# A two-layer decoder block: the last MLP slice as a plain product, the shared key and query gains folded into the weights, and the first attention's maxima as spare contraction rows

## The reference

```python
def _fox_attention(h, w_in, b_f, g_q, g_k, w_out):        # layer 0, 16 heads of 64
    proj = h @ w_in                                       # q, k, v and a gate per head
    q, k = _rmsnorm(q, g_q), _rmsnorm(k, g_k)
    c = cumsum(log_sigmoid(gate + b_f))
    s = q @ k.T * 64 ** -0.5 + c[t] - c[s]                # causal
    return softmax(s) @ v @ w_out

def _shared_kv(h, g_kv, w_kv, g_k):                       # after layer 0
    kv = _rmsnorm(h, g_kv) @ w_kv                         # 128 key and 128 value columns

def _swa_sink_attention(h, w_q, g_q, k_band, v_band, ...) # layer 1, 16 heads, window 128
    q = _rmsnorm((h @ w_q).reshape(...), g_q)
    ...                                                   # scores with bias and sink, softmax, @ v

def _sq_relu_mlp(h, w_up, w_down):
    return square(relu(h @ w_up)) @ w_down                # 1024 -> 4096 -> 1024

for layer in range(2):
    h = h + attention(_rmsnorm(h, g_attn[layer]), ...)    # fox in layer 0, sliding window in layer 1
    h = h + _sq_relu_mlp(_rmsnorm(h, g_mlp[layer]), w_up[layer], w_down[layer])
```

## Time and profile before

| | |
|---|---|
| executions timed | 1196.8, 1198.57 and 1202.5 us, median 1198.57 us |
| the profiled execution | 1199.23 us, of which the span of the trace is 1197.4 us |
| PE busy | 1147.1 us, 96% of the span |
| DVE, POOL, ACT busy | 908.0, 736.2 and 619.5 us |
| mean granted TensorE clock | 0.989 |

### The profile page before, as it was taken

One profiled execution on the slowest core, in us unless ns is written; L12 is line 12 of the kernel. 1 busy time (PEld: TensorE's weight loads), 2 busy tenths in 40 slices (PEclk: granted clock), 3 DMA queues, 4 the chain that ended last, 5 costly groups with the idle time before them and its releaser, 6 DMA issues.

```text
span 1197.4 us, 14655 instructions
## 1 busy us (share of the span) xinstructions
PE 1147.1 (96%) x5282; PEld 942.9 (79%) x5282; DVE 908.0 (76%) x991; ACT 619.5 (52%) x880; POOL 736.2 (61%) x489
## 2 busy tenths in 40 slices
PE   7999999998999999999987799998999999999996
PEld 6778788877888888888865588887888888888884
DVE  6678788866587876877699778876577768776878
ACT  3458788854444444444433588874354344444432
POOL 5515434415588788878856333324487888788856
PEclk9999999998999999999999899999999999999999
DMA  7221211112432423242133201111424233323121
GB/s 242 72 71 36 71 35 35 65 41 71 166 98 88 141 75 118 89 139 73 36 105 106 71 18 54 36 36 47 137 99 141 71 109 102 123 89 100 41 71 71
DMA packets 88498, 101.46 MB, mean 85 GB/s; under 512 B 3640, under 2 KB 68336, under 8 KB 88432
## 3 DMA queue, kind: packets, MB, share of 16 engines
q1 hardware_dynamic: 88224, 100.37, 25.7%
q10 hardware_dynamic: 208, 0.23, 0.1%
HBM read 98.47 MB, written 2.12 MB: 84 GB/s over the span
## 4 chain that ended last, share of the span: by engine, by line
PE 74%; issue 9%; POOL 8%; DVE 7%; ACT 2%; DMA 0%; POOLq 0%; DVEq 0%; ACTq 0%
PE ps L1640 22%; PE ps L1642 22%; PE ps L1641 22%; POOL w_lo L569 4%; PE ps L2110 2%; POOL fox_sq_lo L576 2%; DVE m_nat L1385 1%; DVE xn_lo L1133 1%; POOL ring_lo L613 1%; PE ps L1817 1%; POOL w_lo L613 1%; ACT w_hi L669 1%; PE ps L2073 1%; PE ps L2092 0%; PE ps L2095 0%
## 5 line engine op out<-in xcount | busy, mean ns | idle before, releaser
L613 POOL TENSOR_TENSOR w_lo<-d_raw,w_hi 128x512 fp32r<-128x512 f32 x160 | 253.8, 1613 | 70.3 <-ACT w_hi L862 70.3
L1640 PE MATMUL ps<-xn_hi,w_hi 128*128 128x512 f32 x480 | 192.0, 400 | 2.9 <-DVE xn_lo L1133 2.9
L569 POOL TENSOR_TENSOR w_lo<-stage,w_hi 128x512 fp32r<-128x512 f32 x80 | 119.1, 1520 | 116.6 <-ACT w_hi L669 116.6
L1642 PE MATMUL ps<-xn_hi,w_lo 128*128 128x512 f32 x480 | 187.6, 391 | 0.0
L1641 PE MATMUL ps<-xn_lo,w_hi 128*128 128x512 f32 x480 | 187.3, 390 | 0.0
L862 ACT ACTIVATE w_hi<-d_raw 128x1024 fp32r<-128x1024 f32 x80 | 84.0, 1057 | 126.3 <-PE ps L1642 92.3
L1640 PE MATMUL ps<-w_hi,rows_hi 128*128 128x512 f32 x320 | 125.2, 391 | 7.2 <-POOL w_lo L613 7.2
L1642 PE MATMUL ps<-w_hi,rows_lo 128*128 128x512 f32 x320 | 124.6, 389 | 0.0
L1641 PE MATMUL ps<-w_lo,rows_hi 128*128 128x512 f32 x320 | 124.5, 389 | 0.0
L613 POOL TENSOR_TENSOR w_lo<-stage,w_hi 128x512 fp32r<-128x512 f32 x72 | 104.2, 1478 | 26.7 <-ACT w_hi L862 26.7
L613 POOL TENSOR_TENSOR ring_lo<-stage,ring_hi 128x512 fp32r<-128x512 f32 x56 | 88.9, 1617 | 42.1 <-ACT ring_hi L862 42.1
(11 more groups left out here) (259 smaller groups left out, 2776.5 us busy)
## 6 DMA issues: line engine op xcount, KB each, us to landing
stage<-in_w_up SPq DMA_DIRECT2D x32, 1024.0 KB, 5.2
d_raw<-in_w_down SPq DMA_DIRECT2D x64, 512.0 KB, 3.5
stage<-in_w_in_a SPq DMA_DIRECT2D x16, 512.0 KB, 4.4
stage<-in_w_out_a SPq DMA_DIRECT2D x4, 1024.0 KB, 4.7
stage<-in_w_q_b SPq DMA_DIRECT2D x4, 1024.0 KB, 5.0
stage<-in_w_out_b SPq DMA_DIRECT2D x4, 1024.0 KB, 4.8
stage<-in_w_in_a SPq DMA_DIRECT2D x3, 1024.0 KB, 4.9
x_in<-in_x SPq DMA_DIRECT2D x4, 512.0 KB, 5.3
```

The source lines that it names most:

```text
L569: ins = nc.gpsimd.tensor_tensor(w_lo[:, s, c], stage[:, s, c], w_hi[:, s, c].bitcast(F32), ALU.subtract)
L613: ins = nc.gpsimd.tensor_tensor(lo[:, c], raw[:, c], hi[:, c].bitcast(F32), ALU.subtract)
L1640: mm(out_, st_hi, mv_hi, start=start, stop=False)
L1642: return mm(out_, st_lo, mv_hi, start=False, stop=stop)
```

## The change

**The last MLP slice** of each layer is an ordinary block product: four row blocks A11, A12, A21, A22, four weight blocks, four output blocks of 24 matmuls each, added over both halves inside the accumulator. The sums S and T and their splits are gone there, and two matmul groups of 12 more than before are made for each two blocks.

**Gains in the weights.** `g_kv` and `g_attn[1]` are multiplied into the rows of the staged weights (`scale_rows`, 8 ACT instructions of 128x256 for each unit, in place, before the unit's split). The stream is then split once (`FILL_KV`) and used for both projections; `FILL_Q` is gone.

**Maxima as contraction rows.** The matmuls of `diag` with ones are gone. The negated maxima of the 4 query blocks are kept as a running sum in `fox_shift` (128x4 for each head), turned by a small matmul (`fox_turn`, 128 columns) and written by DVE into 4 partitions of `qk_hi` that the contraction did not use; 4 partitions of ones on the key side add them. `fox_shift` has 8 rows of 4 in memory, of which 2 are used, so that it takes 128 bytes; the gate rows start at partition 16.

```diff
-LAST_ORDER = ("P1", "P6", "P2", "P4", "P7", "P5", "P3")
+LAST_ROWS = {"A11": 0, "A12": 2, "A21": 1, "A22": 5}
+LAST_BLOCKS = ("B11", "B21", "B12", "B22")
+LAST_ADDS = ("U2 to C12", "U2 to C2", "C11", "C21", "C12", "C22 top", "C22 low")
...
+            def scale_rows(u, gain):
+                act.wait_ge(landed[u % 2], 16 * land_count(landing(u)))
+                for k in range(KC):
+                    c = slice(k * 2 * P, (k + 1) * 2 * P)
+                    ins = nc.scalar.activation(stage[:, u % 2, c], stage[:, u % 2, c], ACT.Identity,
+                                               scale=gains[:, 8 * gain + k:8 * gain + k + 1])
+                ins.then_inc(rows_scaled, 1)
+                act.wait_ge(rows_scaled, u - U_KV + 1)
+            def split_q(v):
+                u = U_Q + v
+                scale_rows(u, GAIN_Q)
+                split(land_count(landing(u)), u, u % 2)
...
-            for c in range(2):
-                query_hi(c)
             norm_rstd(2)
-            for c in range(2, KC):
-                query_hi(c)
...
                     dve.wait_ge(fox_max_ready, 2 * j + e + 1)
-                    after(dve, fox_scores_done, 2 * j - 1 + e)
-                    V.tensor_tensor(diag[:, e, :].rearrange("p (b n) -> p b n", b=TB),
-                                    ident[:, None, :].to_broadcast([P, TB, P]),
-                                    nm[:, e, :, None].to_broadcast([P, TB, P]), ALU.mult).then_inc(fox_diag_ready, 1)
+                    V.tensor_tensor(fox_shift[:, e, :], fox_shift[:, e, :].bitcast(F32), nm[:, e, :], ALU.add
+                                    ).then_inc(fox_shift_ready, 1)
+                for e in range(2):
+                    dve.wait_ge(fox_shift_turned, 2 * j + e + 1)
+                    rows = slice(64 - 64 * e, 64 - 64 * e + TB)
+                    V.tensor_tensor(qk_hi[rows, 0, e, :].rearrange("p (b n) -> p b n", b=TB),
+                                    ps[0:TB, SCORE_BANKS[e][0], None, 0:P].to_broadcast([TB, TB, P]),
+                                    ident[0:TB, 0:TB, None].to_broadcast([TB, TB, P]), ALU.mult).then_inc(fox_rows_ready, 1)
...
+                    if turn_before is not None and k == KC - 2:
+                        fox_turn(turn_before, 0)
...
+            def fox_turn(j, e):
+                pe.wait_ge(fox_shift_ready, 2 * j + e + 1)
+                mm(ps[0:TB, SCORE_BANKS[e][0], 0:P], fox_shift[:, e, :], ident_r[:], start=True, stop=True
+                   ).then_inc(fox_shift_turned, 1)
...
-                    pe.wait_ge(fox_diag_ready, 2 * j + e + 1)
+                    pe.wait_ge(fox_rows_ready, 2 * j + e + 1)
...
-                        mm(o, ones_r[:], diag[:, e, qs], start=False, stop=False)
...
-                proj_pair(i, s, 1, (i, 0))
+                proj_pair(i, s, 1, (i, 0), i - 1)
+                fox_turn(i - 1, 1)
...
+            def last_block(layer, name, banks):
+                for sub in range(2):
+                    for half in range(2):
+                        rows, block = f"A{name[1]}{half + 1}", f"B{half + 1}{name[2]}"
+                        key = ("D", LAST, block)
+                        pe.wait_ge(rows_lo_ready, rows_count(layer, LAST, rows))
+                        pe.wait_ge(operand_lo_ready, operand_count(layer, key))
+                        ...
             def down_last(layer):
...
+                last_block(layer, "C11", (2, 3))
+                pe.wait_ge(product_added, add_count(layer, LAST - 1, "P4"))
+                last_block(layer, "C21", Z)
+                pe.wait_ge(product_added, add_count(layer, LAST - 1, "P3"))
+                last_block(layer, "C12", Y)
...
-            for n in range(4, KC):
-                h_lo(FILL_KV, n)
+                h_lo(FILL_KV, n)
+            for n in range(KC):
                 norm_add(2, n, n % 2)
```

More of the change, by code:

```diff
@@ L59 @@
 DOWN_ORDER = ("P1", "P5", "P2", "P6", "P3", "P4", "P7")
-LAST_ORDER = ("P1", "P6", "P2", "P4", "P7", "P5", "P3")
+LAST_ROWS = {"A11": 0, "A12": 2, "A21": 1, "A22": 5}
+LAST_BLOCKS = ("B11", "B21", "B12", "B22")
 ADDS = ("P1 to C11", "P1 to U2", "P5", "P2", "P6", "P3", "P4", "P7")
[L62 to L67, removed]
+LAST_ADDS = ("U2 to C12", "U2 to C2", "C11", "C21", "C12", "C22 top", "C22 low")
+LAST = SLICES - 1
 def mlp_operands(layer):
@@ L79, in down @@
     def down(i):
-        for p, slot in zip(down_order(i), (3, 4, 5, 0, 1, 2, 3) if i == SLICES - 1 else (2, 3, 4, 5, 0, 1, 2)):
-            seq.append((("D", i, PRODUCTS[p][1]), swap[slot]))
+        if i == LAST:
+            blocks = zip(LAST_BLOCKS, (3, 4, 0, 1))
+        else:
+            blocks = zip([PRODUCTS[p][1] for p in DOWN_ORDER], (2, 3, 4, 5, 0, 1, 2))
+        for block, slot in blocks:
+            seq.append((("D", i, block), swap[slot]))
     up(0)
@@ L508, in load_down @@
                     sp.wait_ge(xn_ready, KC * ([FILL_OUT_A, FILL_OUT_B][layer] + 1))
-                for block, last in (("B12", "T2"), ("B22", "B22"), ("B21", "T4"), ("B11", "T3")):
+                blocks = LAST_BLOCKS if i == LAST else ("B12", "B22", "B21", "B11")
+                for block, last in zip(blocks, ("T2", "B22", "T4", "T3")):
                     if i:
                         sp.wait_ge(operand_lo_ready, operand_count(layer, ("D", i - 1, last)))
-                    n = BLOCK[block]
+                    n = LAST_BLOCK[block] if i == LAST else BLOCK[block]
                     r, c = int(block[1]) - 1, T * (int(block[2]) - 1)
@@ L551, in store @@
                 sp.dma_start(dst[:, b:b + n, c:c + T], m_nat[:, b:b + n, c:c + T]).then_inc(out_stored, 16)
-            store(0, 2, 0, "P2")
-            store(2, 2, 0, "P7 to C21")
-            store(2, 2, T, "P5 to C22")
-            store(0, 1, T, "P3 top")
-            store(1, 1, T, "P3 low")
+            store(0, 2, 0, "C11")
+            store(2, 2, 0, "C21")
+            store(0, 2, T, "C12")
+            store(2, 1, T, "C22 top")
+            store(3, 1, T, "C22 low")
             sp.wait_ge(out_stored, 16 * 5)
@@ L1022, in swa_rec, with split_late @@
                 reciprocal(q_rec[:], qkn[:, 1, :], swa_recip_step, j)
[L1024 removed]
+            def split_late(v):
                 u = U_Q + v
[L1026 removed]
+                if v < PAIRS // 2:
+                    split_q(v)
+                else:
+                    split(land_count(landing(u)), u, u % 2)
             def hankel_hi(j):
@@ L1453, in mlp @@
                     rows_low(layer, 0, n)
-                for i in range(last):
+                for i in range(LAST):
                     rows_sum(layer, i, "S4")
@@ L1629, in _ @@
             mlp(1)
-            for name in LAST_ADDS[9:]:
+            for name in ("C12", "C22 top", "C22 low"):
                 add_last(1, name)
@@ L2008, in _ @@
             for k in range(KC):
-                if k == 4:
-                    pe.wait_ge(product_added, add_count(0, last, "P3 low"))
-                    for n in range(4, KC):
+                if k in (2, 3):
+                    pe.wait_ge(product_added, add_count(0, LAST, "C22 low"))
+                    for n in range(2 * k, 2 * k + 2):
                         turn_mlp(n)
```

265 lines of the change are left out of this document (132 added, 133 removed).

## The result

The changed kernel takes 1204.33 us (median of 15 executions, 1202.18 to 1205.95), the kernel before 1198.8 us (15 executions). The ratio is 1.0043, with a 95% interval of 1.0033 to 1.0052: slower by 0.3 to 0.5%, just inside the 0.5% that the prediction called no change, 16 us above its 1188 and 9 us above the top of its range.

The account below looks back on a forecast made before the run. PE was taken to bound the kernel, busy for 1147.1 of 1197.4 us. Terms -7.1 - 9.1 + 1.0 + 7.0 - 2.5 gave -10.7 us, so 1188 us; own range 1184 to 1192, stated range 1180 to 1195.

Parts of the forecast that it names:

- The last slice: Last MLP slice, both layers: sums and POOL wait gone, 72 matmuls run without a stop in 16.3 us; -7.1 us.
- Between the layers: From the first layer's last slice to the first rough scores: earlier norm matmul and second head sum; -9.1 us.
- the allowance for the clock: Between the layers: 1.0 us added for one of three longer idle stretches whose slow clock is not hidden.
- The scaling: Scaling weight units on ACT: 3.4 us a unit (2.5 to 5.2), on the path between the layers and in second attention.
- rival C: Scaled instructions cost as much as ones of 512 columns, 1.8 us more in each of three places: 1193.5; chance 0.15.
- rival B: Second attention: the scaling is hidden because ACT's order leaves room; -7.0 us, 1181; chance 0.10.
- The second attention: Scaling units 2 and 3 delays ACT's diagonal tiles, PE stands 6.1 us, plus 0.9 for the clock; +7.0 us.
- my 0.9 for both: Second attention: 0.9 us allowed because two idle stretches of 3 us may lower PE's clock.
- The first attention: Diagonal products removed, but the chain through POOL and the new wait hide most of PE's saving; -2.5 us.
- rival D: First attention: row products block with POOL, PE stands 2.5 us in each of seven steps; +17.5, 1208; chance 0.05.
- Rival A: First attention: the saving comes whole as POOL's chain shortens like PE's; -8.1 in place of -2.5, 1182; chance 0.15.

Follow-up runs that it names:

- the area back: The changed kernel with fox_shift laid in a free gap inside the area, so that the area starts at its old address: 1189.44 us, ratio to before 0.9913.

## Why the prediction was wrong, step by step

**The step that failed** is the one that all the others rest on: "Elsewhere PE is fed, and there each matmul counts: three of 512 columns start within 0.68 us, 0.227 us each". It was read from before and kept for after. The change moves `area` by 128 bytes, and 2070 matmuls start 6.05 ns later each. That is 12.5 us that neither the sum nor any of the rivals has; shown by undoing it (14.9 us less) and by doing it alone to the kernel before (14.2 us more). The 14.9 hold the 12.5 and some 1.4 for the pairs on one side (1951 x 0.7 ns); the rest, 1.0, is no more than one slow stretch of the clock in another place makes. With the area back the kernel takes 1189.44 us against my 1188, and the table above shows it within 2 us of the forecast at every place. A part of that closeness is luck: the trace of before has a slow stretch in the output projection, which takes 41.73 us at a clock of 0.92 and 38.88 with the area back at 1.00, and these 2.85 us, which no term has, make up for most of what came out too dear elsewhere in it: 2.0 us between the layers and 0.9 in each attention.

**The last slice.** Right in mechanism and size. 16.3 us were forecast; 16.67 with dearer matmuls, 16.32 with the area back (609.23 to 625.55). No wait of PE for POOL is left there. In layer 1, from the start of the slice to the end of the last add, 23.22 us, and 22.71 with the area back, against 30.35: -7.6 where the term is -7.1.

**Between the layers.** Right in mechanism, 1 to 2 us short (54.1 us forecast from `turn_mlp` to the rough scores, 55.4 and, with the area back, 56.1 measured). PE's timeline in the changed kernel:

```profile
633.50 1.91 PE L2032 MATMUL ps<-kept,m_nat 128*128 128x128 f32 x16
...
659.77 2.08 PE L1691 MATMUL ps<-rst,kept 128*128 128x512 f32 x2 [4.53 <-DVE rst L1141]
666.70 1.12 PE L2102 MATMUL ps<-sqt,kept 128*128 128x512 f32 x2 [0.22 <-ACT sqt L1010]
679.12 2.07 PE L2102 MATMUL ps<-sqt,kept 128*128 128x512 f32 x2 [6.71 <-ACT sqt L1010]
688.92 0.65 PE L2122 MATMUL ps<-kd_hi,q_hl 128*128 128x256 f32 x4
```

From `turn_mlp` the norm's matmul comes after 26.3 us (26.7 forecast, 27.8 before), the head sums after 33.2 (32.7) and 45.6 (44.2), the scores after 55.4 (53.1 without the allowance for the clock). The two matmuls at 659.77 take 2.08 us, those of before 1.02: 1.2 against 2.4 GHz. Both long stops, 4.53 and 6.71 us, end in a slow stretch, and I had allowed for one. The time from the last head sum to the scores, which I had taken over as 8.86 us, was 9.80, and 10.41 with the area back.

**The scaling.** Right in size and place. ACT's timeline in turn 0 and 1 of the second attention:

```profile
704.77 3.29 ACT L978 ACTIVATE stage<-stage,gains 128x256 f32<-128x256 f32 x8
...
710.44 2.43 ACT L1092 ACTIVATE swa_diag<-kept,nm 128x128 fp32r<-128x128 f32 x8
...
724.64 3.29 ACT L978 ACTIVATE stage<-stage,gains 128x256 f32<-128x256 f32 x8
```

and PE's, at the exact scores of pairs 1 and 2:

```profile
712.92 0.50 PE L2141 MATMUL ps<-q_hl,kd_hi 128*128 128x512 f32 x1 [2.64 <-ACT swa_diag L1092]
...
714.71 0.63 PE L2141 MATMUL ps<-q_hl,kd_hi 128*128 128x512 f32 x1
...
733.31 0.50 PE L2141 MATMUL ps<-q_hl,kd_hi 128*128 128x512 f32 x1 [3.10 <-ACT swa_diag L1092]
```

Eight scaled instructions take 3.29 us (3.4 forecast), so rival C is out; and PE stands for 2.64 and 3.10 us where 2.8 and 3.3 were forecast, so rival B is out. The page of the Trainium skill that I weighed (ScalarE: Activation LUTs, section What ACT_TABLE_LOAD costs) had been read only in half: it also says that such instructions in a row overlap by about 93 ns, and with that its figures give an estimate of 3.3 us. The trace agrees with that.

**The second attention.** +7.0 forecast, +9.9 measured, +7.9 with the area back. The windows of turns 1, 2 and 3 (from one exact score to the next) in the changed kernel:

```profile
712.92:733.31 20.39, 17.29 (x93) 14.72 (x93) 12.49 (x21) 17.11 (x35) 8.02 (x7) 0.92 0.15 52
733.31:750.44 17.13, 17.13 (x92) 14.90 (x93) 11.92 (x20) 12.90 (x27) 5.88 (x5) 0.90 0.13 44
750.44:765.91 15.47, 15.47 (x94) 13.53 (x92) 13.20 (x22) 13.10 (x26) 4.72 (x4) 1.00 0.06 21
```

and with the area back:

```profile
705.55:724.39 18.84, 15.70 (x92) 13.60 (x92) 12.52 (x21) 17.15 (x35) 8.06 (x7) 1.00 0.17 57
724.39:741.48 17.09, 17.09 (x93) 14.94 (x94) 11.91 (x20) 12.90 (x27) 5.87 (x5) 0.90 0.13 43
```

The stops themselves are alike (2.64 and 3.10, 2.68 and 3.14 us). In the changed kernel a stretch at 1.2 GHz follows both, with the area back only the second. A slow one costs 1.6 to 1.7 us (20.39 - 18.84; 17.13 - 15.47), so my 0.9 for both was too little: 3.3 and 1.7. By the Trainium skill's TensorE: Matmul & The Clock Gate, section The HAM clock gate, the slow clock is the default, activity releases it and idle time brings it back. From rows I had made of that up to 1.8 us a stop. Three of these four stops agree.

**The first attention.** -2.5 forecast, -1.6 in the changed kernel, about -3 with the area back (its own trace -1.6, with 1.6 lost to the clock). The bounds of the term were summed wrongly: its own parts give -0.7 to -4.9, not -1 to -4.5, which changes nothing here. One step of the changed kernel, DVE's timeline:

```profile
159.18 1.31 DVE L1316 TENSOR_TENSOR fox_shift<-fox_shift,nm 128x4 fp32r<-128x4 f32 x1
...
162.12 0.87 DVE L1316 TENSOR_TENSOR fox_shift<-fox_shift,nm 128x4 fp32r<-128x4 f32 x1
163.03 1.39 DVE L1321 TENSOR_TENSOR qk_hi<-ps,kept 4x512 fp32r<-4x512 f32 x2
```

POOL's:

```profile
159.18 5.03 POOL L593 TENSOR_TENSOR w_lo<-stage,w_hi 128x512 fp32r<-128x512 f32 x4 [0.58 <-ACT w_hi L693]
164.39 1.29 POOL L600 TENSOR_TENSOR fox_sq_lo<-sqt,fox_sq_hi 128x512 fp32r<-128x512 f32 x1 [0.18 <-ACT fox_sq_hi L783]
```

and PE's:

```profile
163.05 0.22 PE L1825 MATMUL ps<-ident_r,fox_shift 128*4 128x128 f32 x1 [0.35 <-DVE fox_shift L1316]
163.86 0.47 PE L1839 MATMUL ps<-qk_hi 128*128 128x512 f32 x1 [0.58 <-DVE qk_hi L1321]
...
167.10 0.45 PE L1795 MATMUL ps<-fox_sq_hi,blk_r 128*128 128x512 f32 x1
```

POOL gained more than the 0.45 us I gave it: 5.03 and 1.29 in place of 5.95 and 1.75, and it is done at 165.68, 1.4 us before PE needs it. So the chain through POOL is no longer last; the new one is, from the shift (1.31 and 0.87 us beside POOL) over turn and row product to the scores. A step takes 22.9 to 23.0 us where its first shift takes 1.26 to 1.31 us beside POOL, 21.9 to 22.0 us where it takes 0.16, and the last one 22.3. Both kinds occur in both versions. The row products take 0.69 each beside POOL, so rival D is out. Rival A would have every step near 21.7 us; of the seven steps four come close to it with the area back and two in the changed kernel; the others do not. The size came out near for a reason that was half wrong.

## What to carry to other kernels

When a change adds or resizes any buffer, write down which tiles move against which, and treat that as a part of the change with a bound of its own: here a displacement of 32 bytes (1203.91 against 1189.44 us) outweighs every single term of the sum. Look first at the busy time of the engine that bounds: if it rises while its work falls, compare the mean of the same matmul by pair of tiles before looking at waits. For matmuls like these, keep the operand tiles at distances of whole multiples of 256 bytes, or lay small buffers behind them.

A cost that stands on the wrong engine is worth moving, but look at what it collides with there: the scaling of three units cost 10.9 us on ACT, and on POOL some 2 us (1180.37 against 1178.5 without it) once most of it was placed where DVE was waiting.

## What the runs showed of the hardware that was not expected

Matmuls in a row (128x128 held, 128x512 moving, 4 bytes an element) whose two SBUF tiles were displaced against each other by 32, 128 or 384 bytes started 5.4 to 6.4 ns later one after another (233 against 227 ns, 2.7%); it was so for each of the three pairs `xn, w`, `w, rows` and `xn, ring` that were displaced. Displacements of 256 and 512 bytes did not show it, and a common displacement of all tiles by 128 did not. Matmuls with both tiles on one side lost up to 0.8 ns as well in the same programs; why, no run shows.

A stop of PE of about 3 us was at times followed by a stretch at 1.2 GHz and at times not, in the same place of the program (2.64 us: yes; 2.68 us: no), so that two traces differ by 1.6 us at such a place. That the layout decides it is not shown: executions of one kernel also differ in their mean granted clock (0.987 to 0.991 with the area back).
